# Three of the eight tiles of a 31-tap depthwise convolution made by GpSimd instead of VectorE, in a three-block fp32 kernel

## The reference, cut to what matters

```python
proj = h @ w_in
qkv, z, a, bt, glu, gates = jnp.split(proj, offs, axis=-1)
qkv = jax.nn.silu(causal_depthwise_conv(qkv, gdn_conv_qkv))      # 4 taps, 3072 channels
...
o = chunk_gated_delta_rule(q, k, v, g, beta)                      # needs all of qkv
...
c_lin, c_gate = jnp.split(glu, 2, axis=-1)
c = c_lin * jax.nn.sigmoid(c_gate)
c = causal_depthwise_conv(c, conv_dw_w) + conv_dw_b               # 31 taps, 1024 channels
c = jax.nn.silu(layer_norm(c, conv_ln_g, conv_ln_b))
```

## Time and profile before

| | |
|---|---|
| median of the runs | 4665.0 us (4654.95 to 4666.55) |
| time of the profiled execution | 4662.94 us |
| its span, first to last instruction | 4661.2 us |
| mean granted TensorE clock | 0.963 of full |
| PE busy | 94% of the span |
| DVE busy | 56% |
| ACT busy | 17% |
| POOL busy | 4% |

### The profile page before, as it was taken

How to read it: one execution, slowest core, us unless ns; L and a number is a source line. 1 busy time by engine, 2 the same in 40 slices (tenths; PEclk the granted TensorE clock), 3 DMA queues, 4 the chain that set the end, 5 groups by cost and what they waited for, 6 DMA issues and landing times.

```text
span 4661.2 us, 66675 instructions
## 1 busy us (share of the span) xinstructions
PE 4386.1 (94%) x29036; PEld 3303.7 (71%) x29036; DVE 2631.8 (56%) x4595; ACT 807.4 (17%) x1450; POOL 171.2 (4%) x280
## 2 busy tenths in 40 slices
PE   8999999999998999799999999998999988889899
PEld 7887445577886888456555548885888776777757
DVE  5674877354545446556244336555655538777736
ACT  0001012221022000221122110001100014444311
POOL 0000000010000000000000000000000002222100
PEclk9998998999998999899999999998999999999999
DMA  7532452103321222111211122212222210000021
GB/s 246 176 107 54 71 68 60 28 2 85 97 82 63 91 91 82 54 46 37 72 37 37 46 72 82 90 64 90 82 73 91 73 50 2 2 2 2 11 91 54
DMA packets 284068, 310.37 MB, mean 67 GB/s; under 512 B 7169, under 2 KB 277633, under 8 KB 280705
## 3 DMA queue, kind: packets, MB, share of 16 engines
q1 hardware_dynamic: 283776, 306.11, 22.6%
HBM read 303.99 MB, written 2.10 MB: 66 GB/s over the span
## 4 chain that ended last, share of the span: by engine, by line
PE 49%; DVE 5%; ACT 1%; issue 1%; DMA 0%; SPq 0%; DVEq 0%; ACTq 0%
PE ps L375 22%; PE ps L299 11%; PE ps L2263 1%; PE ps L3158 1%; PE ps L344 1%; PE ps L851 1%; PE ps L866 1%; PE ps L882 1%; PE ps L503 1%; PE ps L1983 1%; PE ps L1972 1%; PE ps L3089 1%; PE ps L3078 1%; DVE tmp L3101 0%; PE ps L3457 0%
## 5 line engine op out<-in xcount | busy, mean ns | idle before, releaser
L375 PE MATMUL ps<-main 128*128 128x256 f32 x5440 | 1206.6, 379 | 0.0
L375 PEld LDWEIGHTS ps<-main 128*128 128x128 f32 x5440 | 1032.9, 190 | 141.2
L299 PE MATMUL ps<-main,w 128*128 128x512 f32 (+1 forms) x2528 | 1111.2, 596 | 22.3 <-DMA w<-in_ffn_wg 12.3
L375 PE MATMUL ps<-main,w 128*128 128x256 f32 x4100 | 917.7, 380 | 7.5 <-DMA w<-in_w_in 4.4
L299 PEld LDWEIGHTS ps<-main,w 128*128 128x128 f32 x2528 | 483.2, 195 | 573.5 <-issue 545.3
L375 PEld LDWEIGHTS ps<-main,w 128*128 128x128 f32 x4100 | 780.2, 190 | 119.1 <-DMA w<-in_w_in 4.6
L467 DVE TENSOR_TENSOR main<-main,ps 128x512 f32<-128x512 f32 x175 | 120.3, 688 | 428.2 <-PE ps L375 427.9
L414 ACT COPY main<-ps 128x256 f32<-128x256 f32 x109 | 40.6, 372 | 935.6 <-PE ps L375 935.6
L464 DVE TENSOR_TENSOR main<-main,ps 128x512 f32<-128x512 f32 x109 | 74.8, 686 | 220.8 <-PE ps L375 218.0
L694 DVE SCALAR_TENSOR_TENSOR main<-main,params_sb 128x512 f32<-128x512 f32 x256 | 192.5, 752 | 9.1
L472 DVE TENSOR_TENSOR main<-main,ps 128x512 f32<-128x512 f32 x175 | 120.3, 687 | 80.2 <-PE ps L375 78.0
(11 more groups left out here) (480 smaller groups left out, 4759.7 us busy)
## 6 DMA issues: line engine op xcount, KB each, us to landing
w<-in_w_in SPq DMA_DIRECT2D x58, 1024.0 KB, 6.3
w<-in_e_w_in SPq DMA_DIRECT2D x28, 1024.0 KB, 5.1
main<-in_ada_w SPq DMA_DIRECT2D x24, 1024.0 KB, 5.0
w<-in_ffn_wg SPq DMA_DIRECT2D x22, 1024.0 KB, 6.4
w<-in_ffn_wu SPq DMA_DIRECT2D x22, 1024.0 KB, 6.5
w<-in_o_w_in SPq DMA_DIRECT2D x20, 1024.0 KB, 5.4
w<-in_ffn_wd SPq DMA_DIRECT2D x16, 1024.0 KB, 5.2
w<-in_w_up SPq DMA_DIRECT2D x16, 1024.0 KB, 5.3
```

The costliest lines, as they stand in the source:

```text
L299: i = pe.mm(PS[b][:, 0:n], wv[:, k, f * 128:(f + 1) * 128], g.X(kg + k), start=kg + k == 0, stop=kg + k == g.nk - 1)
L375: t = pe.mm(PS[b][:, 256 * half:256 * half + 256], weight[:, m, :], x(m), start=m == 0, stop=m == n - 1)
```

## The change

Pool gets a new piece, `pool_mixers`, at the head of its list. It makes tiles 1, 3 and 5 of the long convolution, one after the other. A tap is now two instructions: a product of the shifted tile with the tap's weight into one of two scratch tiles (`C31`), and an addition of that to the sum in `Yc`. Each addition waits for its product. DVE keeps tiles 0, 2, 4, 6, 7: numbers 0 and 2 after "glu lin" 1 and 5, numbers 4, 6 and 7 after f = 0, 2 and 4.

```diff
+    C31 = [mem(36608 + 512 * i, 1)(0) for i in range(2)]
...
+    def pool_mixers(p):
+        s = sem["pool", "conv"]
+        for f in (1, 3, 5):
+            p.wait_ge(*at("out", "glu lin", f))
+            p.wait_ge(*at("cp pad"))
+            p.ts(Yc(f), Cp(f)[:, 0:TOK], par("conv_dw_w", f), par("conv_dw_b", f), MUL, ADD).then_inc(
+                p.inc(s, "tap", 0, "conv31", f), 1)
+            for j in range(1, 31):
+                if f > 1 or j > 2:
+                    p.wait_ge(*at("tap", *((j - 2, "conv31", f) if j > 2 else (j + 28, "conv31", f - 2))))
+                p.ts(C31[j % 2], Cp(f)[:, j:j + TOK], par("conv_dw_w", 8 * j + f), None, MUL).then_inc(
+                    p.inc(s, "tap product", j, f), 1)
+                p.wait_ge(*at("tap product", j, f))
+                p.tt(Yc(f), Yc(f), C31[j % 2], ADD).then_inc(p.inc(s, "tap", j, "conv31", f), 1)
+            p.also("conv31", f)
...
     def dve_mixers(v):
...
-            if f % 2:
+            if f in (1, 5):
                 conv31(f // 2)
...
-            if f in (0, 2, 4, 5):
-                conv31((4, 0, 5, 0, 6, 7)[f])
+            if f in (0, 2, 4):
+                conv31((4, 0, 6, 0, 7)[f])
...
     def pool_program(eng):
         p = Engine("pool", eng, at)
         p.wait_ge(tables, 48)
+        pool_mixers(p)
         pool_gdn(p)
```

## The result

The changed kernel takes 4684.5 us (median of 4 runs, 4680.4 to 4687.0); the kernel before took 4662.2 beside it. The ratio is 1.0048, with a 95% interval of 1.0034 to 1.0061: slower by 16 to 28 us. The forecast was 4697 (its own range 4679 to 4722). The profiled execution has a span of 4685.2 us for 4661.2.

A forecast was written before the change was run, and what follows sets the result against it. PE, busy 94%, was taken as the bound, with DVE hidden under it. A +40.4 us delay at f = 5, less the tail's 8.7 of idle, made +31.8: 4697; own range 4679 to 4722, 8 in 10 4672 to 4732.

The forecast's parts named there:

- turns at SBUF: A DVE instruction with two SBUF inputs and a reading Pool instruction alternate, each costing the other its reading time; DVE loses 0.55.
- The addition's times: Beside DVE, a tap ends 0.55 us after Pool's instruction; a full addition ends 0.94 to 1.12 after DVE's.
- 1.36 us each for 0.783: DVE makes two instructions in a Pool tap of 2.72 us, so each takes 1.36 us; a long tile costs 42.2 us.
- steps 1 to 5: DVE and Pool from 477.9: PE waits 15.9 us for "glu lin" 7, Pool done at 714, copy of q = 10 at 729.1.
- Pool's end: Pool finishes its three tiles at 714, with taps of 2.72 us beside DVE and some 2.0 alone.
- rival C: Dearer turn: whole instructions exclude each other, or Pool's product costs far over an addition; +85 us, 4750; 12%.
- step 8: Mean and "ab" end at 834.1 for 802.26 before; the tail's 8.7 us of idle are gone; sum +31.8 us.
- The bounds: The same chain with lower and higher holds: 1.25 us for a DVE instruction gives +16, 1.57 gives +57.
- both at the upper hold, 1.57: High bound: product as dear as an addition, 1.57 us for a DVE instruction, +57 us.
- +93.6: Rival C's delay with f = 5 at 782, at 1.7 us for a DVE instruction; less 8.7 it gives +85.
- the lower bound: Product 0.46 of hold, addition 0.94, 1.25 us for a DVE instruction: f = 5 at 713, +16 us.
- The ceiling: PE can gain at most the 6.30 and 2.44 us of idle time in the tail, 8.7 us.

The follow-up runs named there:

- additions alone: The changed kernel with Pool making 90 additions with two SBUF inputs, each straight after the last, and no products: 4672.9 us for 4666.5 before.
- first-tap kernel: The changed kernel, but Pool makes only the first tap of tiles 1, 3 and 5, the other 30 left out: 4655.8 us for 4663.9 before.
- the fills: The changed kernel with Pool making three fills of 128x512 in place of each tap's two instructions: 4642.4 us for 4666.5 before.
- the kernel with all long tiles summed in PSUM: The changed kernel with all five of DVE's long tiles summed in PSUM, one bank set aside: 4668.2 us for 4661.3 before.
- Pool beside the kernel before: The kernel before, all eight tiles on DVE, with Pool making 93 products and 93 additions into unread scratch: 4727.7 us for 4663.9.

## Why the prediction was right, and where it was off

- **The cause** was right: turns at SBUF, read from two stretches of the trace before. DVE's delay is 0.31 us at a product and 0.88 at an addition; a sum in PSUM takes no part, and fills delay only the first taps.
- **The addition's times** held. The tap that meets it ends 0.55 after it, as predicted; the addition ends 1.12 us after the DVE instruction ahead of it, the upper of the two values given. Beside additions alone both values come, 0.95 and 1.13.
- **The mis-sized term** is the "1.36 us each for 0.783" that steps 1 to 5 are built on. It has the product hold DVE up for a turn of 0.59 us, as long as it works itself, by a row of another instruction of 0.73 us. The product takes 1.56 us alone and 1.99 beside DVE, but holds DVE up by 0.31. So DVE makes three taps in a Pool tap, not two: 1.18 us each, and a long tile takes 35.6 to 37.1 us with its first tap, not 42.2. PE starts q = 0 at 570.66, 10.1 us late and not 15.9, and f = 5 at 713.6 for 729.1.
- **Pool's end** was wrong the other way, by the same error: 783, not 714, since a tap takes 3.55 us for 2.72 beside DVE and 2.89 for 2.0 alone. The last long tile of DVE, which I had at 0.783 a tap, was stretched too, and gave the third wait, 6.55 us ahead of f = 7 for the copy of q = 16, which no step had. The sign that I had given for rival C, Pool still at work at 780, came without C's price: a long Pool instruction is not a long hold.
- **The sum**: f = 5 starts 24.9 us later (predicted 40.4), the third wait adds 6.55, the tail's 8.74 of idle are gone as in step 8, and PE's work between f = 5 and the spread takes 1.4 more: +24.1. Predicted +31.8. That the two lie so near is in part luck: f = 5 was forecast 15.5 us too late, and the third wait, which no step had, gave 6.55 of that back.
- **The bounds.** The upper one, "both at the upper hold, 1.57", does not come out: with 1.12 us for product and addition it is (2 x 0.55 + 2 x 1.12) / 2 = 1.67, nearly rival C's 1.7 and its +85. (C's own +93.6 is 93.3 by its f = 5 at 782.) The measured time lies nearer the lower bound.
- **The ceiling** of 8.7 us for the gain counted PE's idle time alone. The median of the first-tap kernel agrees (8.1); at the spread its trace and that of the fills are 16.5 and 13.3 us earlier than before, at a higher granted clock in the first (0.98 for 0.96), so the ceiling is not shown to be one.
- The Trainium skill's page SBUF — State Buffer, section "Who interferes with whom", also says that a DVE instruction with at most one SBUF input, outside DVE's two-port modes, does not contend; the 145 taps summed in PSUM agree. The first taps, with one SBUF input too, were held up when they wrote SBUF; the traces do not name modes, so whether they are that exception is not shown. The page's "whole instruction", written there of the two-port modes, does not describe the product: a tap begun 0.60 us into one of 1.99 us ended 0.33 us before it did (563.92 to 564.98, beside 563.32 to 565.31).

## What to carry to other kernels

Before giving work to a second engine, look for a stretch in which both engines already run and compare one instruction's time in and out of it: two heights of the same instruction (0.75 and 1.22 us here) price the sharing, and what the moved work costs the neighbour must stay below what it spares it. Price an engine's instruction twice, its length (when is that engine done) and its hold on what is shared (what does the neighbour lose); the two are not the same number. Work that the bound engine hides has a small ceiling of gain, here 8.7 us of idle time, and no such limit for the loss.

## What the runs showed of the hardware beyond the expectations

- Pool's product, a TENSOR_SCALAR on 128x512 with no column but the weight's, takes 1.56 us alone, more than the two-input addition (1.26), yet costs a concurrent DVE tap 0.31 us where the addition costs 0.72 to 0.88. Pool's first tap, a TENSOR_SCALAR of the same size with a weight and a bias column, takes half of that. In the kernel with all long tiles summed in PSUM:

```profile
L1186 POOL TENSOR_SCALAR main<-main,params_sb x3: 766/767/768, 477.7 to 660.0; 128x512 f32<-128x512 f32 x3
L1191 POOL TENSOR_SCALAR main<-main,params_sb x90: 1555/1566/1999, 478.5 to 749.5; 128x512 f32<-128x512 f32 x90
```

  It is not the shift: with Pool beside the kernel before, the products at j = 0 take 1.56 us or more as well. Whether it is the second column or the tile written is open, and a product with a bias of zero was not tried.
- Beside additions issued one behind the other, DVE's taps come in pairs of 1.47 and 1.64 us, as the addition ends 0.95 or 1.13 us after the tap ahead of it; why there are two values is open.
- The granted clock was lower where PE waited: 0.66 over the 15 us from 560 with the first wait, for 1.00 in the kernel before and in that with the first tap only. From 575 to 776 it was 0.93 with waits and 0.96 in the kernel before without; the kernel with the first tap only, also without, had 0.98 (to 770), so not every difference here comes from waits.
